# A new prologue order: squares summed by TensorE, other transfer order, the fourth memory chunk beside the first projection chunk

## What is computed

```python
# first block
mod = silu(c) @ w_ada + b_ada                  # 24 chunks of w_ada; the first 8 give shift1, scale1
h = rms_norm(x, g_norm1) * (1 + scale1) + shift1
proj = h @ w_in                                # 13 chunks
...
# second block, needed later but computed in the prologue
mem_n = rms_norm(mem, mem_norm_g)
mkv_a = mem_n @ a_mem_kv                       # keys and values, 2 chunks
mkv_b = mem_n @ b_mem_kv                       # keys and values, 2 chunks
```

## Time and profile before

| What | Value |
|---|---|
| Median of 3 runs | 1056.46 us (1056.38 to 1060.5) |
| The profiled execution's own time | 1062.2 us |
| Its span on the core | 1060.4 us |
| PE busy | 1024.4 us, 97% of the span |
| DVE busy | 733.3 us, 69% |
| ACT busy | 562.1 us, 53% |
| HBM read | 183.29 MB, 174 GB/s over the span |
| Mean granted TensorE clock | 0.994 of full speed |

### The profile page before, as it was taken

How to read it: one execution, slowest core, us unless ns; L and a number is a source line. 1 busy time by engine, 2 the same in 40 slices (tenths; PEclk the granted TensorE clock), 3 DMA queues, 4 the chain that set the end, 5 groups by cost and what they waited for, 6 DMA issues and landing times.

```text
span 1060.4 us, 22984 instructions
## 1 busy us (share of the span) xinstructions
PE 1024.4 (97%) x10004; PEld 971.0 (92%) x10004; DVE 733.3 (69%) x1194; ACT 562.1 (53%) x858; POOL 0.9 (0%) x7
## 2 busy tenths in 40 slices
PE   7999999999999999998899999999999999999996
PEld 6898888999999988987779999999998799999996
DVE  4897658899976667887547655666757765665654
ACT  4456374665655548764236444454667655444531
POOL 0000000000000000000000000000000000000000
PEclk9999999999999999999999999999999999999999
DMA  9977545466645563331004555456224445554541
GB/s 349 406 262 299 195 163 217 173 227 253 226 144 191 201 229 120 123 119 42 4 2 167 197 194 198 138 192 229 100 76 136 171 151 195 176 188 160 191 165 40
DMA packets 31237, 185.82 MB, mean 175 GB/s; under 512 B 3473, under 2 KB 4769, under 8 KB 13985
## 3 DMA queue, kind: packets, MB, share of 16 engines
q1 hardware_dynamic: 31136, 184.36, 48.8%
HBM read 183.29 MB, written 1.05 MB: 174 GB/s over the span
## 4 chain that ended last, share of the span: by engine, by line
PE 85%; DVE 6%; ACT 3%; DMA 3%; issue 2%; SPq 1%; DVEq 0%; ACTq 0%
PE banks L383 46%; PE banks L1386 17%; PE banks L348 3%; PE banks L380 2%; PE banks L660 1%; DVE wlo L328 1%; DMA land<-in_mkv_a 1%; PE banks L1929 1%; PE banks L1570 1%; ACT whi L313 1%; PE banks L1919 1%; DMA raw<-in_a_in 1%; PE banks L595 1%; DVE adac L579 1%; PE banks L663 1%
## 5 line engine op out<-in xcount | busy, mean ns | idle before, releaser
L328 DVE TENSOR_TENSOR wlo<-raw,whi 128x2048 fp32r<-128x2048 f32 (+3 forms) x163 | 323.0, 1982 | 168.7 <-ACT whi L313 168.3
L313 ACT ACTIVATE whi<-raw 128x2048 fp32r<-128x2048 f32 (+3 forms) x163 | 270.7, 1663 | 110.7 <-PE banks L1386 75.6
L383 PE MATMUL banks<-h_lo,whi 128*128 128x256 f32 x1376 | 175.1, 279 | 0.0
L383 PE MATMUL banks<-h_hi,whi 128*128 128x256 f32 x1360 | 173.4, 280 | 0.1
L383 PE MATMUL banks<-h_hi,wlo 128*128 128x256 f32 x1376 | 173.2, 278 | 0.0
L383 PEld LDWEIGHTS banks<-h_lo,whi 128*128 128x128 f32 x1376 | 164.0, 187 | 3.2 <-issue 2.6
L383 PEld LDWEIGHTS banks<-h_hi,whi 128*128 128x128 f32 x1360 | 163.3, 189 | 2.3 <-issue 1.2
L383 PEld LDWEIGHTS banks<-h_hi,wlo 128*128 128x128 f32 x1376 | 163.8, 187 | 1.5 <-issue 1.2
L1412 ACT ACTIVATE u<-u 128x256 f32<-128x256 f32 x44 | 18.4, 418 | 124.9 <-DVE u L1466 124.9
L1386 PE MATMUL banks<-m_lo,whi 128*128 128x256 f32 x528 | 74.1, 279 | 0.0
L1386 PE MATMUL banks<-m_hi,whi 128*128 128x256 f32 x528 | 73.9, 279 | 0.0
(11 more groups left out here) (453 smaller groups left out, 1410.2 us busy)
## 6 DMA issues: line engine op xcount, KB each, us to landing
raw<-in_ada SPq DMA_DIRECT2D x24, 1024.0 KB, 6.6
raw<-in_w_up SPq DMA_DIRECT2D x22, 1024.0 KB, 4.8
raw<-in_a_gu SPq DMA_DIRECT2D x22, 1024.0 KB, 4.8
raw<-in_b_gu SPq DMA_DIRECT2D x22, 1024.0 KB, 4.9
raw<-in_w_in SPq DMA_DIRECT2D x12, 1024.0 KB, 6.8
raw<-in_w_down SPq DMA_DIRECT2D x16, 704.0 KB, 4.0
raw<-in_a_in SPq DMA_DIRECT2D x11, 1024.0 KB, 6.9
raw<-in_a_down SPq DMA_DIRECT2D x16, 704.0 KB, 4.1
```

Source lines behind the costliest of these rows:

```text
L313: act.activation(hi_s[k % NSPLIT][:, 0:w], raw[n % NRAW][:, 0:w], ACT.Copy).then_inc(*hi_made.tick(k))
L328: dve.tensor_tensor(lo_s[s][:, 0:w], raw[n % NRAW][:, 0:w], hi_s[s][:, 0:w].bitcast(F), SUB).then_inc(*lo_made.tick(k))
L383: i_ = pe.matmul(b[0:m, j * T:(j + 1) * T], a[:, kt * step + j * m:kt * step + j * m + m], x[:, kt, :], start=st, stop=sp)
```

## The change

Only the prologue and the first pass of the first projection chunk change.

1. DVE no longer adds squares. `pe_mean8` sums all eight tiles by eight fp32 matmuls against the ones, for the memory and for `X`.
2. The memory and mkv 0 come in two halves each, not in four quarters. Then follow ada 0, the small constants, ada 1, `X`, ada 2, mkv 1, ada 3, ada 4, mkv 2, ada 5, ada 6, ada 7, `w_in` 0, mkv 3. Before it was ada 0, ada 1, constants, mkv 1, `X`, ada 2, ada 3, mkv 2, ada 4, ada 5, mkv 3, ada 6, ada 7, `w_in` 0. The large constants move behind one more `w_in` chunk.
3. PE's order is written out anew. Ahead of the sums of ada 5, 6 and 7 stand 4, 8 and 8 matmuls of `pe_spin`; the two at the end stay.
4. mkv 3 is multiplied inside the first pass of the first projection chunk: its 16 fp32 matmuls take the place of the 14 idle ones.
5. ACT makes the memory's factor before it squares `X`, and evacuates mkv 1 after ada 4's part; DVE evacuates mkv 0 before ada 2, scales `X` before ada 3, and evacuates mkv 2 after ada 7.

```diff
@@ pe_chunk, first pass of the first projection chunk
-                        if kt < nk - 1:
-                            for j in range(n_j):
-                                pe.matmul(beside[0:m, j * T:(j + 1) * T],
-                                          a[:, kt * step + j * m:kt * step + j * m + m], x[:, kt, :],
-                                          start=True, stop=True)
+                        for _ in range((1, 2, 2, 2, 2, 2, 2, 3)[kt]):
+                            next(beside, None)
@@ the sum of squares
-        def dve_square8(dve, tag):
-            q = squares[tag]
-            dve.wait_ge(*sq_a.at((tag, 1)))
-            dve.tensor_tensor(q[:, 0:4, :], q[:, 0:4, :], q[:, 4:8, :], ADD).then_inc(*sq_v.tick((tag, 0)))
-            dve.wait_ge(*sq_v.at((tag, 0)))
-            dve.tensor_tensor(q[:, 0:2, :], q[:, 0:2, :], q[:, 2:4, :], ADD).then_inc(*sq_v.tick((tag, 1)))
-
         def pe_mean8(pe, tag, b):
-            pe.wait_ge(*sq_v.at((tag, 1)))
-            pe.matmul(b[:, 0:T], C("ones"), squares[tag][:, 0, :], start=True, stop=False)
-            pe.matmul(b[:, 0:T], C("ones"), squares[tag][:, 1, :], start=False, stop=True).then_inc(*rs_p.tick(tag))
+            for kt in range(8):
+                if kt % 4 == 0:
+                    pe.wait_ge(*sq_a.at((tag, kt // 4)))
+                x = pe.matmul(b[:, 0:T], C("ones"), squares[tag][:, kt, :], start=kt == 0, stop=kt == 7)
+            x.then_inc(*rs_p.tick(tag))
@@ act_one
             act_ada(act, 1)
+            act_rs(act, "mem", bank[5], rs_m)
             act.wait_ge(*d_x.at(0))
             act_square8(act, "n1", X)
-            act_rs(act, "mem", bank[5], rs_m)
             act_ada(act, 2)
+            act_rs(act, "n1", bank[6])
             act_ada(act, 3)
-            act_rs(act, "n1", bank[6])
+            act_ada(act, 4)
             act_evac1(act, 1)
-            for i in range(4, 8):
+            for i in range(5, 8):
                 act_ada(act, i)
@@ dve_one
             dve_ada(dve, 0)
-            dve_square8(dve, "mem")
             dve_ada(dve, 1)
-            dve_square8(dve, "n1")
+            dve_evac1(dve, 0)
             dve_ada(dve, 2)
             dve_rs_column(dve)
-            dve_evac1(dve, 0)
-            dve_ada(dve, 3)
...
-            dve_ada(dve, 4)
-            dve_ada(dve, 5)
+            for i in range(3, 8):
+                dve_ada(dve, i)
             dve_evac1(dve, 2)
-            dve_ada(dve, 6)
-            dve_ada(dve, 7)
@@ pe_one
             pe_wake(pe)
-            for c in range(NM):
-                if c >= 2:
-                    wait_evac1(pe, c - 2)
-                for n, _ in enumerate(pe_mkv(pe, c)):
-                    pe_extra(pe, c, n)
+            drain(pe_mkv(pe, 0))
+            pe.wait_ge(*d_con0.at(0))
+            pe_mean8(pe, "mem", bank[5])
+            pe_ada(pe, 0)
+            pe_ada(pe, 1)
+            pe_mean8(pe, "n1", bank[6])
+            pe_rs_column(pe)
...
+            pe_spin(pe, bank[4], 4)
+            pe_ada(pe, 5)
+            pe_spin(pe, bank[4], 8)
+            pe_ada(pe, 6)
+            pe_spin(pe, bank[4], 8)
+            pe_ada(pe, 7)
             pe_spin(pe, bank[4], 2)
-            two = [pe_own(pe, NM), pe_own(pe, NM + 1)]
+            wait_evac1(pe, 1)
+            last = pe_mkv(pe, 3, 1)
+            two = [pe_own(pe, NM, last), pe_own(pe, NM + 1)]
```

More of the change, by code:

```diff
@@ L181, in build @@
         d_par, d_con0, d_con, d_x = (sig(f"landed_{n}", 16) for n in ("par", "con0", "con", "x"))
-        d_mem, d_wfg = [sig(f"landed_mem{i}", 16) for i in range(4)], sig("landed_wfg", 16)
-        d_mkv0 = [sig(f"landed_mkv0_{i}", 16) for i in range(4)]
+        d_mem, d_wfg = [sig(f"landed_mem{i}", 16) for i in range(2)], sig("landed_wfg", 16)
+        d_mkv0 = [sig(f"landed_mkv0_{i}", 16) for i in range(2)]
         d_mkv = [sig(f"landed_mkv{i}", 16) for i in range(1, 4)]
@@ L525, in build @@
         mbank = bank[7]
-        WHEN_CON = ("w_in", 2)
+        WHEN_CON = ("w_in", 4)
         S1z = S1[:, :, :, :].rearrange("p a c (b f) -> p (a c) b f", b=2)
@@ L644, in dve_rs_column, with pe_mkv @@
             dve.tensor_copy(rs_c, bank[4][:, 0:2]).then_inc(*misc_v.tick("column"))
-        def pe_mkv(pe, c):
+        def pe_mkv(pe, c, piece=4):
             w, b = mkv_w[c], bank[c % 2]
@@ L654, in pe_mkv @@
             for o, (j, kt) in enumerate(turns):
-                if c == 0 and o % 4 == 0:
-                    pe.wait_ge(*d_mkv0[o // 4].at(0))
+                if c == 0 and o % 8 == 0:
+                    pe.wait_ge(*d_mkv0[o // 8].at(0))
                 if c == 0 and j == 0:
@@ L666, in pe_mkv @@
                     x.then_inc(*mkv_done.tick(ONE[c]))
-                if o % 4 == 3:
+                if o % piece == piece - 1:
                     yield
@@ L1168, in pe_extra, with pe_own @@
                     pe_gsq(pe, e[1])
-            if c == 1 and piece == 0:
-                pe.wait_ge(*d_con0.at(0))
-                pe_mean8(pe, "mem", bank[5])
-            if c == 1 and piece == 3:
-                pe_mean8(pe, "n1", bank[6])
-                pe_rs_column(pe)
-            for i in EARLY_SUMS.get((c, piece), ()):
-                pe_ada(pe, i)
             if piece == 3 and 5 <= c <= 16 and c - 1 in ADA_AT:
                 pe_ada(pe, ADA_AT[c - 1])
-        def pe_own(pe, c):
+        def pe_own(pe, c, beside=None):
             name, i = ONE[c]
@@ L1185, in pe_own @@
                                 (name, i) in TOK1, wait_h("n1") if c < NM + 2 else None,
-                                beside=bank[4] if c == NM else None)
+                                beside=beside)
         def pe_spin(pe, b, n):
@@ L1199, in pe_one @@
             pe_wake(pe)
-            for c in range(NM):
-                if c >= 2:
-                    wait_evac1(pe, c - 2)
-                for n, _ in enumerate(pe_mkv(pe, c)):
-                    pe_extra(pe, c, n)
+            drain(pe_mkv(pe, 0))
[5 more added lines that the diff above has]
+            pe_rs_column(pe)
+            second = pe_mkv(pe, 1)
+            next(second)
+            next(second)
+            pe_ada(pe, 2)
+            drain(second)
+            pe_ada(pe, 3)
+            wait_evac1(pe, 0)
+            third = pe_mkv(pe, 2)
+            next(third)
+            next(third)
+            pe_ada(pe, 4)
+            drain(third)
+            pe_spin(pe, bank[4], 4)
[4 more added lines that the diff above has]
+            pe_ada(pe, 7)
             pe_spin(pe, bank[4], 2)
-            two = [pe_own(pe, NM), pe_own(pe, NM + 1)]
+            wait_evac1(pe, 1)
+            last = pe_mkv(pe, 3, 1)
+            two = [pe_own(pe, NM, last), pe_own(pe, NM + 1)]
             for g, times in ((0, 4), (1, 4), (0, 2), (1, 2)):
@@ L3263, in sp_program @@
                 if n == 0:
-                    for h in range(4):
-                        t2, c2 = slice(2 * h, 2 * h + 2), slice(512 * h, 512 * h + 512)
-                        sp.dma_start(mem[:, t2, :], A["memT"][:, t2, :]).then_inc(*d_mem[h].tick(0))
-                        sp.dma_start(mkv_w[0][:, c2], A["mkv_a"][0][:, c2]).then_inc(*d_mkv0[h].tick(0))
+                    for h in range(2):
+                        t4, c4 = slice(4 * h, 4 * h + 4), slice(1024 * h, 1024 * h + 1024)
+                        sp.dma_start(mem[:, t4, :], A["memT"][:, t4, :]).then_inc(*d_mem[h].tick(0))
+                        sp.dma_start(mkv_w[0][:, c4], A["mkv_a"][0][:, c4]).then_inc(*d_mkv0[h].tick(0))
+                if n == 1:
+                    sp.dma_start(con[:, 0:NFIRST], A["cons"][:, 0:NFIRST]).then_inc(*d_con0.tick(0))
                 if n == 2:
-                    sp.dma_start(con[:, 0:NFIRST], A["cons"][:, 0:NFIRST]).then_inc(*d_con0.tick(0))
+                    sp.dma_start(X[:, :, :], A["xT"]).then_inc(*d_x.tick(0))
+                if n == 3:
                     sp_mkv(sp, 1)
-                    sp.dma_start(X[:, :, :], A["xT"]).then_inc(*d_x.tick(0))
-                if n == 4:
+                if n == 5:
                     sp_mkv(sp, 2)
-                if n == 6:
+                if n == 9:
                     sp_mkv(sp, 3)
```

5 lines of the change are left out of this document (2 added, 3 removed).

## The result

The changed kernel is slower. Its median is 1066.18 us (6 runs, 1063.04 to 1067.38) against 1056.43 us for the kernel before (6 runs, 1055.43 to 1060.5) on the same chip. The ratio is 1.0069, 95% interval 1.005 to 1.0088, which is +7.3 us on 1056.5 (5.3 to 9.3); the two medians lie 9.75 apart. The forecast was +6.8, and 1063.3 as a time.

What follows compares the result with a forecast made beforehand. The prediction took PE as the bound, with the prologue becoming bound by PE alone. Its terms, 2.4 for the prologue, 5.3 for the pass and -0.9 for vanished waits, gave +6.8 on 1056.5: 1063.3 us, range 1059.0 to 1067.0.

Steps and rivals of the forecast that it cites:

- three signs of being wrong: PE waiting ahead of the sums of ada 5 to 7, a pass clearly under 9 us, or `mod` before 48.7.
- Step 1: mkv 0 at the start: PE begins at 8.5 us, when the first half is there, and ends at 15.6.
- Rival C: Quicker start of the stream: halves gain up to 1.3 us; +5.4, 1061.9 us; chance included in the forecast's 0.72.
- rival B: Clock falls in PE's longer pause ahead of mkv 0: 1.9 us lost, +8.7, 1065.2 us; chance 0.12.
- Step 2: The memory's mean behind mkv 0: eight matmuls on PE, 3.6 us, until 19.2.
- Step 3: Factor and squares of `X`: ACT's squares at 21.1 and 22.1, PE's column of factors done at 25.0.
- Step 4: Rest of the prologue, through ada 7's sum: PE alone the bound, 26.1 us, `mod` at 51.1, +2.4 us.
- Rival A: Idle matmuls ahead of ada 5 to 7 are free, filling PE's waits: -0.1, 1056.4 us; chance 0.09.
- Step 5: First pass with mkv 3 inside: 9.0 us instead of 3.71, +5.3 us.
- Steps 6 and 7: Behind the pass: ada 8's part 2.5 us later at no cost; PE's waits for DVE and a bank vanish, -0.9.

Runs made afterwards that it cites:

- e4: The changed kernel with the memory and mkv 0 in quarters, as before the change: 1064.43 us, ratio 1.0056 to the kernel before.
- e5: The kernel before with mkv 3 moved into the first pass, nothing in its old place: 1064.06 us, ratio 1.0049.
- e6: The kernel before with the squares of the memory and of `X` summed by PE, at the old places in its order: 1064.05 us, ratio 1.0051.
- e8: The kernel before with only the memory's squares summed by PE, right behind mkv 0, and small constants ahead of ada 1: 1058.97 us, ratio 1.0.
- e9: The changed kernel without the 20 idle matmuls and with the memory and mkv 0 in quarters: 1059.0 us, ratio 1.0006 to the kernel before.
- e10: e9 with mkv 3 multiplied ahead of ada 7 and out of the first pass: 1062.99 us, ratio 1.0035 to the kernel before.
- e1: The changed kernel without the 20 idle matmuls ahead of the sums of ada 5, 6 and 7: 1060.5 us, ratio 1.0024 to the kernel before.
- e2: The changed kernel with mkv 3 replacing 16 of the 20 idle matmuls and 14 idle ones back in the pass: 1062.63 us, ratio 1.0047.
- e7: The changed kernel with DVE adding the squares again, for the memory and for `X`: 1067.11 us, ratio 1.008 to the kernel before.
- e3: The changed kernel with 13 idle matmuls at the very start instead of 5: 1065.55 us, ratio 1.0061 to the kernel before.

## Why the prediction was right, point by point

The direction and the mechanism held: PE is the bound, and the added fp32 matmuls are paid on its path. None of its three signs of being wrong appeared. The size was near by the ratio (+6.8 against +7.3) and 2.9 us low by the medians (1063.3 against 1066.18), and the trace shows that the terms were less good than the sum.

**Step 1, mkv 0, failed.** Forecast: start 8.5, end 15.6. Measured: 9.18 and 19.1. The first half landed at 1.64 + 7.49 = 9.13 us by the chain of waits:

```profile
1.64 7.49 DMA land<-in_mkv_a
```

The halves came neither at once with the second quarter of before (8.5) nor faster. Rival C, the quicker start, is out. The forecast had read the rule of the Trainium skill, "DMA: Bandwidth & Descriptors", section Bandwidth, to batch transfers to 1 MB or more, as a quicker start too, and the measurement is against that reading. Here PE waits for the first piece that it can use. With quarters it began at 6.0 to 7.2 in all seven traces that have them (before, e4, e5, e6, e8, e9, e10), and with halves at 9.0 to 9.7 in four (after, e1, e2, e7). More weighty is that the step priced all 16 matmuls at full clock. The pause was 3.72 us, not 2.4, because the five idle matmuls took 3.95 us this time instead of 4.63 and the data came later. This is rival B, whose price of 1.9 was 2.8. By the Trainium skill, "TensorE: Matmul & The Clock Gate", part 1, activity releases the throttled clock. The changed kernel's trace agrees: the granted clock is 0.50 when PE begins mkv 0 at 9.18, and 1.00 again from 15 on with PE at work. The forecast used that rule only to say that the 20 idle matmuls buy nothing. They bought 1.6 us in the pass (8.70 against 10.28 in e1). One reading was too sure: the first five idle matmuls do take twice the price, but the trace's granted clock reads 1.00 in that stretch, so that it was the lower clock isn't shown by it.

**Step 2** held: the memory's mean took 3.62 (3.6). **Step 3** had the wait for ACT right in kind (PE idle ahead of the squares of `X`), but not its consequence: a second fall of the clock, 1.8 us, which neither the forecast nor rival B had. The column of factors is done at 30.3, forecast 25.0: 3.5 from step 1, 1.8 from this.

**Step 4** was exact in its length. From the column to the last ada sum it counted 26.1 us; the trace has 30.16 to 56.32, 26.2. So `mod` is at 56.35 instead of 51.1 for the reasons of steps 1 and 3 alone. ada 7 was ready at 47.2, not at 43.3, but PE came to its sum at 55.4, so the slack of the others was 8 us where 7 was forecast. e1 shows the claim directly: without the idle matmuls PE waits 0.50, and 8.0 of their 8.8 us are gone where the forecast had 7 of 8.9 paid. **Rival A** (idle matmuls free) falls with it: its point of decision was PE's end of mkv 2 at 34, and that was at 45.4. Their being paid is what the ratios of e1 and of the changed kernel tell apart.

**Step 5**: 9.0 forecast, 8.70 measured, 8.70 - 3.69 = 5.0 more than with mkv 3 outside (e2). Where the clock was low as it began it was 9.9 to 10.3 (e1, e5, e9).

**Steps 6 and 7**: DVE begins ada 8's part at 68.40, 8.0 us later than before and not 2.5. But 7.6 of that is `mod`'s own shift, and the step had said "no more than `mod`". PE was later still and waited for none of it, so it costs nothing. The waits of PE for DVE behind the pass vanished as said. The pass ended 12.6 us later than before, and 10.7 are left at 85 us: 2.0 came back where 0.9 was expected.

**The sum.** By the trace +10.7 at 85 us, and +9.0 at 132 us, against 6.8. That the forecast still met the ratio was partly luck. The two falls of the clock, which it left out, cost 4.6 us in the profiled execution, and that execution was the slowest of the six; the kernel with more idle matmuls at the start (e3), whose trace has neither fall, is only 0.08% better in its ratio, within its interval. Each taken out alone, the idle matmuls are the largest item (1.0069 to 1.0024, 0.45%; 8.4 us at 85 us), mkv 3 in the pass the second (0.22%; 3.3 us at 85 us), the halves the third (0.13%; 3.2 us at 85 us, part of it a fall of the clock). These don't add up to a sum, since each also changes the waits behind it. The last two differences lie within the intervals.

**What stays open**: how often the falls of the clock come. Only one execution of each kernel was profiled. The mean granted clock of the others says that they differ: of the changed kernel's six executions four have 0.995, at 1063.04 to 1066.57 us, and two have 0.991, at 1066.81 and 1067.38 us, the profiled one among these. After, e1 and e2 have the same PE program up to the column of factors, and in e1 the second fall is missing. Nor was part 2, 3 or 5 of the change tried by itself; e9 shows only that together with parts 1 and 4 they come to nothing.

## What to carry to other kernels

An engine that is 97% busy has no free filler: idle matmuls cost their 0.445 us each, and are worth it only where a wait stands in the trace that is as long as they are. Before work is moved off the bound, ask what is next: here DVE and the memory chunks' transfers were so close behind PE that a gain in its queue turned into waits of 2.0 to 3.3 us (e5, e8, e10), with a lower clock behind each. And an edit has no price of its own: the same squares on PE cost 5.6 us in one order and nothing that the runs can tell in the other.

## What the runs showed of the hardware

- The clock falls not only behind a pause without any work (3.72 us ahead of mkv 0), but also behind two microseconds with PE busy 0.38 and 0.45 of each, and behind waits of 2.0 to 2.4 us for DVE or a transfer (e4, e5, e8). PE then works on at 1.2 GHz: from 9 to 14 and from 25 to 28 in the changed kernel, from 31 to 35 mostly in e8. The price can be as high as the wait or higher: 1.8 us behind the 1.17 us for ACT in the changed kernel, and 1.7 behind the 1.99 us in e8 (4 us at 0.57).
- The same pause can leave the clock alone. 1.17 us for ACT at `X` were followed by the low clock in the changed kernel and in e2 and by the full one in e1 and e3, though after, e1 and e2 have the same PE program up to there. 1.49 us for DVE near 120 us were followed by it in six traces of twelve. So a fall, or its absence, in one trace isn't an effect of the edit until a second trace says so.
- In the pass the clock was low only where no matmuls of 128x256 stood between the last ada sums (e1, e5, e9: 9.9 to 10.3 us with mkv 3 inside). With idle or memory matmuls there it was full.
- The granted clock of the trace doesn't tell the first microseconds. It reads 1.00 from 0 to 8 us in the changed kernel's trace while the first five matmuls took 3.95 us. In e9 it reads 1.00 throughout mkv 0, which took 9.05 us with records of up to 0.80 us against 0.38 as the rule.
- Two transfers of 512 KB each for memory and weights, in turn on one queue, land their first pair at 9.1 us; in quarters of 256 KB PE could begin at 6.0 to 7.2. Here the size of the first pieces set when PE could begin.
- fp32 and fp32r matmuls in turn cost the sum of the two kinds: 16 of the one and 16 of the other in 8.70 us against 9.0 from their groups. The switch itself shows no price.
